# Neighbourhood scores of two heads, formed side by side in the two row halves of TensorE

## What is computed

```python
def neighbourhood_attention(q, k, v, k_ctx, v_ctx, rpb):
    ...
    s_win = jnp.einsum('brqhd,brwkhd->bhrqwk', qg, k_blk).astype(F32) * scale + bias
    s_win = jnp.where(in_win[:, None, :], s_win, -jnp.inf)
    s_ctx = jnp.einsum('brqhd,blhd->bhrql', qg, k_ctx).astype(F32) * scale
    p = jax.nn.softmax(jnp.concatenate([s_win..., s_ctx], axis=-1), axis=-1)
    out = p_win @ v_blk + p_ctx @ v_ctx
```

## Time and profile before

| | us |
|---|---|
| median of 3 runs | 2049.99 (2049.72 to 2051.14) |
| the profiled execution | 2048.59 |
| its span, first to last instruction | 2046.8 |
| TensorE busy | 1641.6 (80%) |
| DVE, ACT, POOL busy | 605.3, 280.9, 122.3 |

### The profile page before, as it was taken

How to read it: one execution, slowest core, us unless ns; L and a number is a source line. 1 busy time by engine, 2 the same in 40 slices (tenths; PEclk the granted TensorE clock), 3 DMA queues, 4 the chain that set the end, 5 groups by cost and what they waited for, 6 DMA issues and landing times.

```text
span 2046.8 us, 26229 instructions
## 1 busy us (share of the span) xinstructions
PE 1641.6 (80%) x10520; PEld 824.2 (40%) x10520; DVE 605.3 (30%) x1186; ACT 280.9 (14%) x581; POOL 122.3 (6%) x135
## 2 busy tenths in 40 slices
PE   7999997756666666666555667999999999999997
PEld 3677775111111111111111114888888433333332
DVE  3887765000000000000000003674603422222222
ACT  3214422000000000000000002214311100000001
POOL 0026412000000000000000001100100000000000
PEclk9999998888878777777888778999999999999999
DMA  9872056999999999999999997577257999999997
GB/s 394 358 262 87 3 217 254 420 432 432 430 433 431 427 436 430 430 430 432 431 431 430 434 433 295 194 307 272 94 208 301 423 426 428 426 428 427 428 427 294
DMA packets 55058, 730.42 MB, mean 357 GB/s; under 512 B 6145, under 2 KB 6593, under 8 KB 11330
## 3 DMA queue, kind: packets, MB, share of 16 engines
q1 hardware_dynamic: 52848, 722.23, 84.3%
q10 hardware_dynamic: 2130, 7.07, 1.0%
HBM read 728.19 MB, written 1.09 MB: 356 GB/s over the span
## 4 chain that ended last, share of the span: by engine, by line
PE 47%; DMA 41%; DVE 7%; issue 2%; ACT 1%; POOL 1%; DVEq 0%; SPq 0%; ACTq 0%; POOLq 0%
DMA ring<-in_w_moe 41%; PE psum L944 9%; PE psum L1150 7%; PE psum L985 5%; PE psum L619 4%; PE psum L965 2%; PE psum L637 2%; PE psum L1523 2%; PE psum L1300 2%; PE psum L1312 1%; PE psum L1326 1%; PE psum L1881 1%; PE psum L919 1%; DVE ring L2737 1%; PE psum L1578 1%
## 5 line engine op out<-in xcount | busy, mean ns | idle before, releaser
L619 PE MATMUL psum<-ring,main 128*32 128x512 f32 x2016 | 324.9, 803 | 193.2 <-DMA ring<-in_w_moe 187.7
L619 PEld LDWEIGHTS psum<-ring,main 128*32 128x32 f32 x2016 | 74.8, 141 | 433.0 <-DMA ring<-in_w_moe 234.7
L637 PE MATMUL psum<-ring,main 128*32 128x512 f32 x1000 | 149.3, 746 | 76.3 <-DMA ring<-in_w_moe 76.3
L679 DVE TENSOR_TENSOR main<-main,psum 128x512 f32<-128x512 f32 x16 | 11.0, 687 | 561.7 <-ACT main L700 561.7
L1150 PE MATMUL psum<-main,ring 128*128 128x256 f32 x768 | 167.6, 379 | 0.0
L944 PE MATMUL psum<-ring,main 128*64 128x512 f32 x688 | 153.8, 594 | 4.6 <-DMA ring<-in_w_moe 4.6
L1150 PEld LDWEIGHTS psum<-main,ring 128*128 128x128 f32 x768 | 145.4, 190 | 19.9 <-issue 0.5
L637 PEld LDWEIGHTS psum<-ring,main 128*32 128x32 f32 x1000 | 33.8, 128 | 175.4 <-DMA ring<-in_w_moe 104.0
L944 PEld LDWEIGHTS psum<-ring,main 128*64 128x64 f32 x688 | 48.7, 137 | 104.6 <-issue 92.2
L682 DVE TENSOR_TENSOR main<-psum,main 128x512 f32<-128x512 f32 x16 | 11.1, 692 | 242.8 <-PE psum L637 242.8
L700 ACT ACTIVATE main<-psum 128x512 f32<-128x512 f32 x16 | 9.6, 597 | 511.5 <-PE psum L619 511.5
(11 more groups left out here) (499 smaller groups left out, 1938.1 us busy)
## 6 DMA issues: line engine op xcount, KB each, us to landing
ring<-in_w_moe SPq DMA_DIRECT2D x70, 4096.0 KB, 23.7
ring<-in_w_moe SPq DMA_DIRECT2D x105, 2048.0 KB, 23.0
main<-in_w_moe SPq DMA_DIRECT2D x20, 2048.0 KB, 29.3
ring<-in_w_in SPq DMA_DIRECT2D x34, 1024.0 KB, 6.4
main<-in_w_moe SPq DMA_DIRECT2D x33, 1024.0 KB, 17.8
ring<-in_w_mod_t SPq DMA_DIRECT2D x24, 1024.0 KB, 6.0
main<-in_w_mod_t SPq DMA_DIRECT2D x16, 1024.0 KB, 8.3
ring<-in_w_moe SPq DMA_DIRECT2D x13, 1024.0 KB, 10.2
```

The lines of the kernel that those rows point to most:

```text
L619: last = mm(psum[32 * j:32 * j + 32, b, :], xg1[:, k, :], w[:, 512 * j:512 * j + 512], start=k == 0, stop=k == KT - 1)
L637: last = mm(psum[q:q + 32, BANK_Y, :], hidT[:, P * (f % 4) + 32 * (f // 4):P * (f % 4) + 32 * (f // 4) + 32], w[:, r, 512 * g:512 * g + 51 ...
```

## The change

The order of the items changes: the two heads of one half pair follow each other for the same query tile. In an even level of the first eight, TensorE requests two banks and forms the scores of items n and n+1, the one with the upper, the other with the lower 64 rows of the array. The odd ones form none. DVE and ACT keep their places: they treat item n in level n.

```diff
-        ATT = [("na", h, t) for h in range(H) for t in range(NT)] + [("df", h, t) for h in range(H) for t in range(NT)]
+        ATT = [("na", h, t) for p in range(H // 2) for t in range(NT) for h in (2 * p, 2 * p + 1)] + [("df", h, t) for h in range(H) for t in range(NT)]
...
                 if kind == "na":
-                    o = banks.new(("s", i, 0))
-                    pe.wait_ge(*banks.free(("s", i, 0)))
+                    for u in range(2):
+                        banks.new(("s", i + u, 0))
+                        pe.wait_ge(*banks.free(("s", i + u, 0)))
                     for f in range(2):
                         pe.wait_ge(*banks.read_out(("in", "na_q", f)))
                         pe.wait_ge(*banks.read_out(("in", "na_k", f)))
-                    last = mm(o[:, :], na_q[hpart(h), h // 2, P * t:P * t + P], na_k[hpart(h), h // 2, :], start=True, stop=True)
-                    last.then_inc(banks.when_full(("s", i, 0)), 1)
+                    for u in range(2):
+                        rows_ = hpart(h + u)
+                        mm(banks.tile(("s", i + u, 0)), na_q[rows_, h // 2, P * t:P * t + P], na_k[rows_, h // 2, :],
+                           start=True, stop=True).then_inc(banks.when_full(("s", i + u, 0)), 1)
...
             def fill_early(n):
-                if n < NA_N:
+                if n < NA_N and (n >= 8 or n % 2 == 0):
                     scores(n)
```

## The result

The changed kernel took 2056.74 us (median of 9 runs, 2054.78 to 2058.2), the kernel before, on the same chip, 2051.12 us (9 runs, 2049.68 to 2051.93): ratio 1.0029, 95% interval 1.0021 to 1.0037. By the ratio that is slower by 5.9 us, more than the 4.35 us of the forecast, and 0.4 us above the high end of its range. Measured a second time, it gave 2055.79 us against 2050.77: 1.0044 (1.0030 to 1.0058). The median of the kernel before had itself moved by 1.13 us, from 2049.99 (3 runs) to 2051.12 (9 runs), more than the 0.4 us by which the forecast's range was left.

The account below looks back on a forecast made before the run. TensorE was taken to bound levels 0 to 7. Terms -0.05 - 0.25 - 0.25 + 2.27 = +1.72 us, plus 2.63 for the clock, gave +4.35: 2054.3 us on the median's level, 0.21% slower, range 2050.9 to 2056.3.

Parts of the forecast that it names:

- The pair at 1.06 us: Levels 0, 2, 4, 6: two scores side by side take 1.06 us together, so these levels stay as they are.
- What the odd levels give back: Without their score, levels 3 and 7 gain 0.25 us each and level 1 gains 0.05, not 1.05 each.
- The bank wait, +2.27: p of level 5 must wait until ACT has read score 5 from its bank: +2.27 us, bounds 0 and 2.5.
- The waits of level 4 and of the query products: Same bank wait for y of level 4 and level 7's query products: both free, up to 1 us each if uncovered.
- What the gap does to the clock, +2.63: TensorE's 3.26 us standstill before p of level 5 halves the clock, slowing y, scores and p: +2.63 us.
- Bounds 0 and 3.4: Limits on the clock's price; 3.4 us is half of a slow stretch of 6.8 us, all on the path.
- the sum's end at level 7: The forecast's sum had terms for levels 0 to 7 and the clock behind level 5's gap, giving +4.35 us.
- The change lies within levels 0 to 7: Claim that in these levels TensorE's time is the kernel's time; DVE and ACT have slack except at bank waits.
- the later fall: Clock fall from 248 us after a 1.97 us gap at 246.78; its absence would give back 2.63 us; chance 0.06.
- Faster by the clock: Rival: the shifted levels avoid the fall at 248, none at level 5: -0.9 us, 2049.1 us; chance 0.06.
- The other rivals: Bank wait without clock 2051.7 us (0.22); no bank wait 2049.2 (0.04); pair in sequence 2057.5 to 2058.5 (0.04); all gained 2045.8 (0.02).
- within 0.2%: Whole kernel: time changes by no more than 0.2%, chance 0.55; slower by more 0.42, faster by more 0.03.

Follow-up runs that it names:

- e9: The changed kernel unaltered, measured and profiled a second time: 2055.79 us against 2050.77 before, ratio 1.0044.
- c1: The changed kernel unaltered, profiled once more for its trace: 2056.29 us, one execution.
- e2: The changed kernel with the exponential of score 5 taken a level early, so p of level 5 finds its bank free: 1.0004 against before, 2050.72 us.
- e5: The changed kernel with pairs for items 0 to 3 only, single scores in levels 4 to 7: 0.9997 against before, 2049.91 us.
- e14: e2 plus TensorE kept running near 317 us, and GpSimd waiting after two of five masks for DVE's probabilities: 0.9986 against before, 2046.12 us.
- e3: The changed kernel with seven unread matmuls filling the gap ahead of p of level 5: 1.0017 against before, 2054.38 us.
- e6: e2 with p of level 7 held up by two unread products: 1.0005 against before, 2050.84 us.
- e12: The changed kernel with three pairs (scores 6 and 7 single), its bank wait kept: 1.0028 against before, 2056.38 us.
- e1: The kernel before, with p of level 5 made to wait until ACT has read score 5, no pairs: 1.0011 against before, 2051.82 us.
- c2: The changed kernel unaltered, profiled once more for its trace: 2057.91 us, one execution.

## Why the prediction was wrong, and where it was right

- **The pair at 1.06 us**: right. Four records, 1.06 us.
- **What the odd levels give back**: right; level 3 0.24 us (forecast 0.25), level 7 0.23 from 14.16 - 13.93, and 19.73 - 19.44 - 0.24 = 0.05 us for level 1, forecast 0.05.
- **The bank wait, +2.27**: right, 8.43 - 6.14 = 2.29 us, in the place and by the releaser named. That it fits to 0.02 us is luck: the bias sum came 0.25 us behind the copies (202.04 against 200.00 + 1.79) where I had it 0.03 behind, and p came 0.10 us behind ACT's read (204.17 against 203.88 + 0.19) where I had 0.30. The waits of level 4 and of the query products weren't felt, as argued.
- **What the gap does to the clock, +2.63**: right as a mechanism, mis-sized, and no constant. The fall came in three of five profiled executions at 3.0 us each (it lasts longer than the y, score and p that I priced), a mean of 1.8 us. "Bounds 0 and 3.4" held it.
- **The step that failed** is the sum's end at level 7. "The change lies within levels 0 to 7" and "the later fall": everything behind counted as a copy of before, but for one rival with 6% in which a fall near 248 us gives 2.63 us back. The five executions of the change against the two of before, by column of the table: levels 1 to 9 +3.7 us (1.77 and the clock, one execution of the five with another 0.74 in level 1 to 5); level 9 +1.9, of which 0.93 is DVE held by GpSimd and the rest the clock behind the longer gap, in all five; levels 13 to 15 +1.4; all else within 0.1. Sum +7.0 us, and another 1.4 us of the same executions lies outside the levels, with no cause found. Up to level 9 the forecast had been 4.35 where 3.7 was measured; the 3.3 us behind it are what it put at nothing. The timed comparisons, 5.9 us (4.3 to 7.6) and 9.0 (6.2 to 11.9), lie around it.
- **Faster by the clock**, -0.9: its price was wrong. In e9 and c1 the fall near 248 did stay away, and nothing was gained, because TensorE isn't what bounds levels 13 and 14. The 1.97 us gap of the earlier trace rows, ahead of that fall, was itself the sign of it: TensorE waits there for ACT.
- The other rivals were out as argued. Of the two sentences of the Trainium skill's page "TensorEngine Tiling (Array Packing)" the first (Theoretical Speedup), up to twofold, holds for the pair itself (1.06 us where two took 2.10). The second (PSUM Bottleneck), that the reading of PSUM gets no faster, agrees too: ACT's copy of y in level 3 took 0.60 us before and after. Of the pair's gain the kernel kept nothing that can be measured: in e2 and e5, where no bank holds p of level 5 up, the ratio is 1.0004 and 0.9997, and the levels up to 9 gave back 0.8 and 0.3 us.
- The direction was right, "within 0.2%" with 0.55 was not.

What a DVE product with both inputs in SBUF waits for is told by the Trainium skill ("SBUF — State Buffer", Who interferes with whom): such an instruction shares its second port with GpSimd's reads, and whichever is issued first keeps it to its end. The traces agree: in the change the small product ends with the third mask, and the two products with two inputs in SBUF took 0.99 and 1.67 us beside the masks and 0.22 and 0.75 without them in e14, while the sum with one input in PSUM (L3097, 0.69 us at 218.33 in the kernel before, under the masks, and 0.69 at 224.66 after them) didn't change.

What stays open: why the 1.58 us gap of level 9 lowered the clock in all five executions of the change and in e3, but not in e2 and e6, which have the same gap some microseconds earlier; and why the change's fall in levels 13 to 15 took the longer or later form each time. All of these have the 2.3 us delay ahead of them, but e12 has it too and lost nothing there. Single executions can't tell a rule from chance here.

## What to carry to other kernels

Forming a result earlier than its reader takes it costs a bank for the time between: before moving a product up, count the requests until its bank comes round again, and read which engine must have emptied it by then. Price a fall of the clock only where TensorE itself bounds, and look at the idle time around the slow stretch to know: where it waited for others here, up to 10.2 us of half clock were free, 13.6 us cost 1.6 us, and 3.4 us placed a little later cost 1.1 us. And a step made 0.2 us earlier can be the one that makes DVE wait for GpSimd: follow what runs beside the next instructions with two inputs in SBUF, also in the levels that the change doesn't touch.

## What the chip showed that I had not expected

- One kernel, one gap of 3.27 us: granted clock 0.50 behind it in three executions, 1.00 in two. A gap of 2.27 us (e1) lowered it, as did 1.97 us; at the same place 1.95 us in e9 and 1.97 us in c1 did not.
- A fall may come late: in c2 p still took 1.16 us right behind the gap, and only the turn after it 1.11 instead of 0.66; in e12 p already took 1.97.
- DVE's product of one column per row, 0.22 us of work, took 0.99 us beside a GpSimd product; 128x512 took 1.50 to 1.67 instead of 0.75.
- Nine products whose result nobody reads (18 records), run while TensorE waits for another engine, made the eight matmuls behind the wait (16 records) take 3.69 instead of 5.57 us.
